# First RMS norm of a two-block transformer kernel: from feature rows to token rows

## What is computed

```python
def rms_norm(x, g, eps=NORM_EPS):
    xf = x.astype(jnp.float32)
    y = xf * lax.rsqrt(jnp.mean(xf * xf, axis=-1, keepdims=True) + eps)
    return (y * g.astype(jnp.float32)).astype(x.dtype)

# first_block, layer 0
h = rms_norm(x, g_mix[layer])
x = x + rwkv7_time_mix(h, rw_mu[i], rw_w_r[i], rw_w_k[i], rw_w_v[i], rw_w_o[i], ...)

# rwkv7_time_mix
h_prev = jnp.pad(h, ((0, 0), (1, 0), (0, 0)))[:, :-1]
hh = h_prev - h
xk = h + hh * mu[2]      # and five more mixes: xr, xw, xv, xa, xg
r = xr @ w_r
```

## Time and profile before

| | us |
|---|---|
| median of 3 runs | 2099.76 |
| lowest and highest | 2094.2 and 2106.43 |
| profiled execution, own time | 2102.84 |
| its span in the trace | 2100.8 |
| TensorE busy in it | 1922.4 (92%), 14984 matmul records |
| VectorE, ScalarE, GpSimd busy | 808.2, 761.6, 777.3 |
| mean granted TensorE clock | 0.962 of full speed |

### The profile page before, as it was taken

How to read it: one execution, slowest core, us unless ns; L and a number is a source line. 1 busy time by engine, 2 the same in 40 slices (tenths; PEclk the granted TensorE clock), 3 DMA queues, 4 the chain that set the end, 5 groups by cost and what they waited for, 6 DMA issues and landing times.

```text
span 2100.8 us, 35512 instructions
## 1 busy us (share of the span) xinstructions
PE 1922.4 (92%) x14984; PEld 1577.2 (75%) x14984; DVE 808.2 (38%) x1298; ACT 761.6 (36%) x1045; POOL 777.3 (37%) x647
## 2 busy tenths in 40 slices
PE   5998987778999999999998899999998999979997
PEld 3667866768788888877776678888887886768877
DVE  5588334445322221029867342222002133223333
ACT  6776233343322222133267232222212423243232
POOL 3354300014444444436321344444444534233442
PEclk8999899899999999999999999999999999889998
DMA  5112000012233333222210123333222311131221
GB/s 170 61 33 86 14 3 4 4 44 82 81 100 100 96 89 105 90 82 88 78 43 21 42 81 98 100 100 95 95 90 81 101 51 51 41 106 61 63 73 46
DMA packets 192357, 149.58 MB, mean 71 GB/s; under 512 B 6890, under 2 KB 190401, under 8 KB 192228
## 3 DMA queue, kind: packets, MB, share of 16 engines
q1 hardware_dynamic: 192228, 147.68, 22.8%
HBM read 145.57 MB, written 2.10 MB: 70 GB/s over the span
## 4 chain that ended last, share of the span: by engine, by line
PE 72%; DVE 11%; issue 7%; ACT 5%; POOL 3%; DMA 1%; SPq 0%; DVEq 0%; ACTq 0%; POOLq 0%
PE psum L2664 20%; PE psum L2666 19%; PE psum L2665 19%; PE psum L2841 4%; POOL w_lo L1201 3%; ACT w_hi L1334 1%; DVE X_lo L1903 1%; PE psum L3140 1%; PE psum L3153 1%; DVE xf L2363 1%; DVE col L2412 1%; DVE tq L2383 1%; PE psum L3250 0%; PE psum L3033 0%; PE psum L3263 0%
## 5 line engine op out<-in xcount | busy, mean ns | idle before, releaser
L1201 POOL TENSOR_TENSOR w_lo<-weight_raw,w_hi 128x256 fp32r<-128x256 f32 (+4 forms) x604 | 732.1, 1243 | 1060.3 <-ACT w_hi L1334 1060.1
L2664 PE MATMUL psum<-X_hi,w_hi 128*128 128x512 f32 x1336 | 551.3, 413 | 38.2 <-DVE X_lo L1903 21.5
L2665 PE MATMUL psum<-X_lo,w_hi 128*128 128x512 f32 x1336 | 527.5, 395 | 0.0
L2666 PE MATMUL psum<-X_hi,w_lo 128*128 128x512 f32 x1336 | 527.4, 395 | 0.0
L1334 ACT ACTIVATE w_hi<-weight_raw 128x2048 fp32r<-128x2048 f32 (+1 forms) x136 | 252.9, 1860 | 321.2 <-PE psum L2666 300.3
L2664 PEld LDWEIGHTS psum<-X_hi,w_hi 128*128 128x128 f32 x1336 | 254.6, 191 | 118.5 <-issue 46.7
L2665 PEld LDWEIGHTS psum<-X_lo,w_hi 128*128 128x128 f32 x1336 | 255.0, 191 | 58.7 <-issue 8.9
L2666 PEld LDWEIGHTS psum<-X_hi,w_lo 128*128 128x128 f32 x1336 | 254.8, 191 | 55.2
L2664 PE MATMUL psum<-w_hi,X_hi 128*128 128x256 f32 x640 | 189.2, 296 | 16.2 <-DVE X_lo L1903 9.0
L2665 PE MATMUL psum<-w_lo,X_hi 128*128 128x256 f32 x640 | 184.4, 288 | 0.0
L2666 PE MATMUL psum<-w_hi,X_lo 128*128 128x256 f32 x640 | 184.3, 288 | 0.0
(11 more groups left out here) (473 smaller groups left out, 2596.9 us busy)
## 6 DMA issues: line engine op xcount, KB each, us to landing
weight_raw<-in_ffn_w_gu SPq DMA_DIRECT2D x88, 512.0 KB, 5.0
weight_raw<-in_l_w_in SPq DMA_DIRECT2D x45, 512.0 KB, 4.7
weight_raw<-in_ffn_w_down SPq DMA_DIRECT2D x40, 512.0 KB, 3.7
weight_raw<-in_kv_w SPq DMA_DIRECT2D x16, 512.0 KB, 4.4
weight_raw<-in_l_w_out SPq DMA_DIRECT2D x16, 512.0 KB, 4.2
weight_raw<-in_rw_w_o SPq DMA_DIRECT2D x12, 512.0 KB, 4.5
weight_raw<-in_rw_w_k SPq DMA_DIRECT2D x8, 512.0 KB, 6.7
weight_raw<-in_rw_w_r SPq DMA_DIRECT2D x8, 512.0 KB, 4.0
```

Source lines behind the costliest of these rows:

```text
L1201: ins = pool.tensor_tensor(l, r, h.bitcast(F32), ALU.subtract)
L2664: pe.matmul(ps, wh, xh, start=start, stop=False, skip_group_check=True)
L2665: pe.matmul(ps, wh, xl, start=False, stop=False, skip_group_check=True)
L2666: return pe.matmul(ps, wl, xh, start=False, stop=stop, skip_group_check=True)
```

## The change

The first RMS norm is computed from `xtok`, where a token is a row. VectorE squares each piece of x as it lands (16 instructions of 128x256) and keeps the sums per token, in four columns per partition. After a reduction, ScalarE's root and a reciprocal on four columns, VectorE writes four diagonal matrices `dg` (the identity times 1/root). TensorE then forms `xtok` times `dg`, which transposes and normalises at once (32 matmuls of 128 columns, jobs ("xh", k)). ScalarE (k even) and VectorE (k odd) multiply by g_mix on the way from PSUM to `h_sb`. The plain transposes to `x` stay, since x is needed as the residual; they use four banks in place of two. The eight squares, the eight sums with ones, the reciprocal of 128x512 and the eight instructions for `h_sb` go.

Besides, the parameter rows are split in two (`pv` 0 with g_mix and mu, `pv` 1 with the rest, transposed ahead of step 1), the identity is loaded ahead of the other constants, ScalarE splits weight slot 0 before it works on h, and slot 1, `first_raw` and `heads_r` later. The tile `xtok` moves to the place of `rf`, so that SyncE waits for the last product with `dg` before it loads `second_raw`.

```diff
     for k in range(KT):
-        j.add(("xt", k), 4 + k % 2, "A")
-    j.add(("rms", 0), 6, "A")
-    j.add(("pv",), 7, "A")
+        j.add(("xt", k), 4 + k % 4, "A")
+    j.add(("pv", 0), 2, "A")
+    for k in range(KT):
+        j.add(("xh", k), (4, 5, 0, 1)[k % 4], "AD"[k % 2])
+    j.add(("pv", 1), 5, "A")
...
+        xtok = here(arena + size([P, KT, S + 1], F32) + size([P, KT, S], F32))("xtok", [P, TT, D])
+        xsq = here(x_at + size([P, KT, S], F32))("xsq", [P, 4, TT, 256])
...
+            sp.dma_start(c_("ident"), t["c_main"][:, CST["ident"]:CST["ident"] + P]).then_inc(ident_in, 16)
+            for i in range(4):
+                sp.dma_start(xtok[:, :, 256 * i:256 * i + 256],
+                             t["x"][0].rearrange("(t p) d -> p t d", p=P)[:, :, 256 * i:256 * i + 256]
+                             ).then_inc(x_in[i], 16)
+            fill_rows(0, ROWS_A)
+            fill(0)
             for i, name in enumerate(("da_lam_q1", "da_lam_k1", "da_lam_q2", "da_lam_k2")):
                 sp.dma_start(lamr[0:1, 64 * i:64 * i + 64], t[name]).then_inc(lam_in, 16)
-            sp.dma_start(heads_f[:, :], t["c_heads"]).then_inc(heads_in, 16)
-            sp.dma_start(keep[:, :], t["c_keep"]).then_inc(keep_in, 16)
+            fill(1)
             for i, name in enumerate(("rw_w1", "rw_a1")):
                 sp.dma_start(first_raw[:, :, 64 * i:64 * i + 64], t[name][0].rearrange("(k p) c -> p k c", p=P)
                              ).then_inc(lora_in[0], 16)
+            sp.dma_start(cst[:, P:NCST], t["c_main"][:, P:NCST]).then_inc(cst_in, 16)
+            fill_rows(1, ROWS_B)
+            sp.dma_start(heads_f[:, :], t["c_heads"]).then_inc(heads_in, 16)
+            sp.dma_start(keep[:, :], t["c_keep"]).then_inc(keep_in, 16)
+            wait_done(sp, ("xh", KT - 1))
...
                 if v == 0:
-                    act.wait_ge(h_ready, k + 1)
+                    if k % 2 == 0:
+                        empty(("xh", k), h_sb[:, k, 1:S + 1], scale=pcol("g_mix", k))
+                    wait_job(act, ("xh", k))
...
+            act.wait_ge(ident_in, 16)
+            act.activation(ybias[:, :], cst[:, 0:TT], ACT.Sqrt)
             for k in range(KT):
                 empty(("xt", k), x[:, k, :])
-            norm_squares(0)
-            wait_done(act, ("pv",))
-            act.activation(pv[:, :], psum[:, 7, 0:P + NROWS_B], ACT.Copy).then_inc(job_a, 1)
+            act.wait_ge(tok_sum, 1)
+            act.activation(ypart[:, :], ypart[:, :], ACT.Sqrt).then_inc(tok_root, 1)
+            wait_done(act, ("pv", 0))
+            act.activation(pv[:, 0:P], psum[:, 2, 0:P], ACT.Copy).then_inc(job_a, 1)
             high(0)
-            high(1)
-            act.wait_ge(heads_in, 16)
-            act.activation(heads_r[:, :], heads_f[:, :], ACT.Copy).then_inc(heads_ready, 1)
+            wait_job(act, ("pv", 0))
+            act.wait_ge(omu_ready, 1)
...
+            def beside_first(k):
+                if k == 0:
+                    high(1)
+                if k == 4:
+                    lora_high(0)
+
+            mix_high(0, MU_K, beside_first)
             lora_high(1)
             ring_first(0)
             ring_first(1)
             for j in range(2):
                 ring_high(j)
+            act.wait_ge(heads_in, 16)
+            act.activation(heads_r[:, :], heads_f[:, :], ACT.Copy).then_inc(heads_ready, 1)
+            wait_done(act, ("pv", 1))
+            act.activation(pv[:, P:P + NROWS_B], psum[:, 5, 0:NROWS_B], ACT.Copy).then_inc(job_a, 1)
+            act.wait_ge(heads_ready, 1)
             keys_out(0)
...
-            wait_done(dve, ("xt", KT - 1))
+            dve.wait_ge(ident_in, 16)
+            for i in range(4):
+                dve.wait_ge(x_in[i], 16)
+                for tt in range(TT):
+                    piece = xtok[:, tt, 256 * i:256 * i + 256]
+                    ins = dve.scalar_tensor_tensor(out=xsq[:, i, tt, :], in0=piece, scalar=1.0, in1=piece, op0=ALU.mult,
+                                                   op1=ALU.mult, accum_out=ysum[:, tt, i:i + 1])
+            link(ins)
+            link(dve.tensor_reduce(ypart[:, :], ysum[:, :, :], AX.X, ALU.add))
+            dve.tensor_scalar(ypart[:, :], ypart[:, :], 1.0 / D, 1e-6, ALU.mult, ALU.add).then_inc(tok_sum, 1)
             dve.memset(h_sb[:, :, 0:1], 0.0)
-            norm_scale(0)
-            wait_job(dve, ("pv",))
-            link(dve.tensor_scalar(omu[:, :], pv[:, PV["rw_mu"]:PV["rw_mu"] + 48], -1.0, 1.0, ALU.mult, ALU.add))
+            dve.wait_ge(tok_root, 1)
+            dve.reciprocal(rstd[:, :], ypart[:, :]).then_inc(tok_inv, 1)
+            dve.wait_ge(tok_inv, 1)
+            for tt in range(TT):
+                ins = dve.tensor_scalar(dg[:, tt, :], c_("ident"), rstd[:, tt:tt + 1], None, ALU.mult)
+            ins.then_inc(dg_ready, 1)
+            wait_job(dve, ("pv", 0))
+            dve.tensor_scalar(omu[:, :], pv[:, PV["rw_mu"]:PV["rw_mu"] + 48], -1.0, 1.0, ALU.mult, ALU.add
+                              ).then_inc(omu_ready, 1)
             link(dve.tensor_scalar(oka[:, :], pv[:, PV["rw_k_a"]:PV["rw_k_a"] + KT], -1.0, 1.0, ALU.mult, ALU.add))
...
-            dve.wait_ge(lam_row, 1)
-            for k in range(KT):
-                dve.scalar_tensor_tensor(out=h_sb[:, k, 1:S + 1], in0=x[:, k, :], scalar=pcol("g_mix", k),
-                                         in1=rt[:, :], op0=ALU.mult, op1=ALU.mult).then_inc(h_ready, 1)
-            dve.wait_ge(h_ready, KT)
+
+            def normed(k):
+                key = ("xh", k)
+                wait_done(dve, key)
+                dve.tensor_scalar(h_sb[:, k, 1:S + 1], bank(job_banks(key)[0]), pcol("g_mix", k), None, ALU.mult
+                                  ).then_inc(job_d, 1)
...
-            split(0, mixed(0, MU_K))
+            def first_mixed(k, f):
+                if k + 3 < KT and k % 2 == 0:
+                    normed(k + 3)
+                return mixed(0, MU_K)(k, f)
+
+            normed(1)
+            split(0, first_mixed)
...
-            pe.wait_ge(cst_in, 16)
+            pe.wait_ge(ident_in, 16)
             for k in range(KT):
                 pe.wait_ge(x_in[k // 2], 16)
                 b = begin(("xt", k))
                 for tt in range(TT):
                     ins = pe.transpose(psum[:, b, P * tt:P * tt + P], xtok[:, tt, P * k:P * k + P], c_("ident"))
                 ins.then_inc(job_done, 1)
+            pe.wait_ge(rows_in[0], 16 * len(ROWS_A))
+            b = begin(("pv", 0))
+            pe.transpose(psum[:, b, 0:P], prow[0][:, :], c_("ident")).then_inc(job_done, 1)
+            pe.wait_ge(dg_ready, 1)
             for k in range(KT):
-                norm_part(0, k)
-            pe.wait_ge(rows_in, 16 * (len(ROWS_A) + len(ROWS_B) + 2))
-            b = begin(("pv",))
-            pe.transpose(psum[:, b, 0:P], prow[0][:, :], c_("ident"))
-            pe.transpose(psum[:, b, P:P + NROWS_B], prow[1][:, :], cst[0:NROWS_B, CST["ident"]:CST["ident"] + NROWS_B]
-                         ).then_inc(job_done, 1)
+                b = begin(("xh", k))
+                for tt in range(TT):
+                    ins = pe.matmul(psum[:, b, P * tt:P * tt + P], xtok[:, tt, P * k:P * k + P], dg[:, tt, :],
+                                    start=True, stop=True, skip_group_check=True)
+                ins.then_inc(job_done, 1)
...
+                if i == 1:
+                    pe.wait_ge(cst_in, 16)
+                    pe.wait_ge(rows_in[1], 16 * (len(ROWS_B) + 2))
+                    b = begin(("pv", 1))
+                    pe.transpose(psum[:, b, 0:NROWS_B], prow[1][:, :],
+                                 cst[0:NROWS_B, CST["ident"]:CST["ident"] + NROWS_B]).then_inc(job_done, 1)
                 features(PL.first["k"] + i, XV["xk"] if i == 0 else None, parts=low_rank(i))
```

More of the change, by code:

```diff
@@ L701, in here @@
             return alloc
-        a_ = here(arena)
-        xtok = a_("xtok", [P, TT, D])
+        xtok = here(arena + size([P, KT, S + 1], F32) + size([P, KT, S], F32))("xtok", [P, TT, D])
+        xsq = here(x_at + size([P, KT, S], F32))("xsq", [P, 4, TT, 256])
+        a_ = here(arena + size([P, KT, S + 1], F32))
         prow = [a_("prow0", [P, P]), a_("prow1", [NROWS_B, P])]
         heads_f = a_("heads_f", [P, D])
-        lamr = a_("lamr", [1, 256])
-        lamp = a_("lamp", [1, 128])
         a_ = here(arena)
@@ L722, in build @@
         pchunk = a_("pchunk", [P, KT, NCH])
+        b_ = here(a_.spot[0])
+        lamr, lamp = b_("lamr", [1, 256]), b_("lamp", [1, 128])
         mid_hi = a_("mid_hi", [P, S], F32R)
@@ L725, in build @@
         midf_at = a_.spot[0]
+        dg = here(midf_at)("dg", [P, TT, P])
         midf = a_("midf", [P, S])
@@ L1106, in fill_ffn, with fill_rows @@
                                          ).then_inc(raw_full[(n0 + j) % 2], 16)
-            sp.dma_start(cst[:, :], t["c_main"]).then_inc(cst_in, 16)
-            for i in range(4):
-                sp.dma_start(xtok[:, :, 256 * i:256 * i + 256],
```

(8 more changed lines are left out.)

25 lines of the change are left out of this document (11 added, 14 removed).

## The result

| | before | after |
|---|---|---|
| median of 7 runs each, us | 2096.97 | 2078.06 |
| lowest and highest | 2094.2 and 2106.43 | 2070.97 and 2084.23 |
| profiled execution, own time | 2102.84 | 2084.23 |
| its span | 2100.8 | 2082.4 |
| TensorE busy in it | 1922.4 | 1914.9 |

The changed kernel takes 0.9905 of the time before (95% interval 0.9879 to 0.9932), 18.9 us less. The two profiled spans differ by 18.4 us, so the traces hold nearly the whole difference. The forecast stood on a median of 2099.76 from three runs of the kernel before; over seven it is 2096.97.

What follows compares the result with a forecast made beforehand. TensorE's 17.3 us wait before product "k" was taken as the bound: starting 12.7 earlier, less 0.3 for parameter rows, gives 12.4, so 2102.84 becomes 2090.4, scaled to the median 2087.4 us; range 2080 to 2095.

Steps and rivals of the forecast that it cites:

- From there on both lists are the old ones ... So the lead is carried to the end: After step 0 of product "k": instruction lists unchanged, so the start's lead, 12.4 us, lasts to the end.
- The base of the sum: Whole kernel: the profiled run's 2090.4 us was scaled to the median of 2099.76, giving 2087.4.
- x lands: Loading at the start: fewer constants queued ahead save 1.6 us; first piece at 4.7, last at 9.4.
- `dg`: VectorE after the root: reciprocal 0.17 and four diagonals of 0.2 each, ready at 13.1 us.
- Products with `dg`: TensorE after the diagonals: four fp32 products per tile take 0.91 us; tile of k=7 ready at 20.8.
- Tiles and mixes: ScalarE and VectorE before product "k": tiles of h at 0.60 and 0.69 us; product "k" begins at 26.5.
- Weight slot 0: Loading behind x: lands at 12.6 us, ScalarE's part ends at 14.6, GpSimd's `w_lo` at 22.2.
- rival 1: Weight loading: slot 0 shares queues with slot 1, landing at 15.7; gain 9.3 us, time 2090.5; chance 0.10.
- rival 2: Work on h and mixes: GpSimd holds VectorE; gain 8.7 us, time 2091.1; chance 0.14 together with Rival 4.
- The cold start: Step 0 of product "k": TensorE starts at the low clock again, lasting 13.1 us; warm would gain 2.3 more.
- rival 3: Steps 0 and 1: clock stays low, 11.7 us slower, time 2111.5; chance 0.04 including a later unseen stall.
- Rival 4: End of step 0: ScalarE's list runs late, the ring starves; gain 8.0 us, 2091.8; 0.14 together with rival 2.

Runs made afterwards that it cites:

- q3: Kernel before with 200 already fulfilled waits on TensorE in its idle stretch ahead of product "k": ratio 0.9946 to the kernel before.
- n1: Kernel before with 99 already fulfilled waits on TensorE in its idle stretch ahead of product "k": 2094.27 us, ratio 0.9968.
- q2: Kernel before with 150 already fulfilled waits on TensorE in its idle stretch ahead of product "k": ratio 0.9965.
- n2: Changed kernel with 158 more fulfilled waits on TensorE, 81 ahead of the transposes and 77 ahead of product "k": 2086.42 us, ratio 0.994.
- p4: Changed kernel with the normalised tiles of h in PSUM banks 4, 5, 2, 3 in place of 4, 5, 0, 1: 2072.64 us, ratio 0.9872.
- r2: Changed kernel with tiles of h in banks 4, 5, 2, 3 and 88 fulfilled waits on TensorE in idle places: 2080.76 us, ratio 0.9919.

## Why the prediction missed

**The step that failed** is "From there on both lists are the old ones ... So the lead is carried to the end". The lists are the same, but TensorE's stands at another place, and the core answers with 6.6 us (profiled pair); I had read the list's contents and not its position. q3, at the same place within two instructions, shows such a gain without the change, as do n1 and q2 at others; n2 takes part of it away with the change in place. Without it the sum would have been 12.4 predicted against 11.4 in the trace, and 2087.4 against 2088.4.

**The base of the sum** was the other part. I scaled to 2099.76, the median of three runs; over seven it is 2096.97, 2.8 less. 2087.4 plus the 1.0 that the start fell short, less 6.6 and 2.8, is 2079.0, against 2078.06 measured. With the base of three runs, the gain of 18.9 would have ended at 2080.9, just inside the range.

**x lands**: predicted 4.7, measured 5.66. Leaving 620 KB out ahead of x brought 0.7 us, not 1.6, since the first piece had come at 6.3: mis-sized. Squares follow each other by 0.35 (0.34 predicted) and end at 11.5 for 10.8, about the late landing.

**`dg`**: reciprocal 0.18 (0.17), four diagonals 0.88 (0.8); ready at 14.2 for 13.1, of which 0.9 is the landing.

**Products with `dg`**: mechanism right, size off. I took 0.91 per tile from a stretch at the upper clock; the clock was 0.68 from 16 to 20, after a pause of 1.84 us, and eight tiles took 9.04, or 1.13 each (in p4 and r2 too). This is the other part of the late start: the last tile is ready at 23.3, not 20.8.

**Tiles and mixes**: tiles of h on VectorE took 0.73 to 0.75 (0.69), on ScalarE 0.67 to 0.69 (0.60), eight small excesses. Product "k" began at 28.33 (26.5), and waited for ScalarE's tile 6 in bank 0, as forecast. It is 0.7 inside the bound named for "wrong" (after 29) and outside the 26 to 27 named for "right"; `kf` came at 41.53 (40).

**Weight slot 0, rival 1**: ScalarE waited 0.54 us for it and began at 13.81 (12.6); `w_lo` was there at 21.3 (22.2). "A wait past 13" was a sign of wrong, and it came true, but 13.81 is 1.2 late, of which x's late landing explains 1.0; sharing with slot 1 would have meant 15.7. The rival fell.

**GpSimd, rival 2**: tiles of h from PSUM were never held (0.73 to 0.75 beside running `w_lo`), two `xf` mixes beside it took 1.21 and 1.22, the other two 0.76 and 0.74. The rule of the Trainium skill on "Who interferes with whom" in "SBUF — State Buffer", weighed in the prediction, has VectorE contend with GpSimd where both its inputs lie in SBUF. By it the `X_lo` of odd k are held: one was, 2.31 us beside `first_lo`, and one a little, 0.87; one was not, 0.68 at 28.63 in the middle of slot 1's `w_lo`. There GpSimd was the slower one, 7.34 us for eight where slot 0 took 5.52. So the rule says where to look, and the trace says who pays.

**The cold start, and rival 3**: the cold start came as forecast (clock 0.50 from 28 to 32, 0.97 from 32 to 36, up at 32.3, 4.0 us after product "k" began), so rival 3, a clock that stays low, fell. The 2.3 us promised for a warm start are not to be had: p4 had it and gained 0.9 at `kf`, because ScalarE's list is next. I had put its cover at 0.6 us, which is near.

**Rival 4** did not come: no wait for `ring_lo` over 1 us, and ScalarE, not the ring, stands next behind TensorE.

The chances (faster 0.63) had the right favourite. The range was built from the start's terms alone, and none of these reached what the core did: 8 to 17 us of gain were allowed, 18.9 came. The start alone, 11.4, lay inside.

## What to carry to other kernels

A change that adds or removes instructions on TensorE shifts all that follows in its list, and a stage of short matmuls far behind can answer with several us either way; read the lead against the kernel before at many points before crediting the edit, and test with fulfilled waits in an idle stretch. Count in the trace how many instructions such an edit adds: here two waits of the source made one, and a plan built on the source's count put most runs at other places than meant. Budget such an effect in a range when gains of 0.5% are weighed. A waiting engine hides the next one: here 5.6 us of earlier start were worth 0.9, because ScalarE's list was right behind.
